# First norm's row factor moved behind the first projection, a new order around sine chains, filter banks, seam and cross heads

## The reference

```python
def first_block(x, ...):
    h = rmsnorm(x, norm_mix)                      # x * rsqrt(mean(x*x)) * gain, per position
    p = h @ w_in                                  # 2048 -> 4352: pool 512, hyena 3*768, gated MLP 2*768
    y_a = multiscale_pool_mixer(p[..., :512], ...)
    h_fwd, h_bwd = implicit_filters(...)          # two sine layers, then w3 times a decay table
    y_b = hyena_mixer(p[...], conv3, h_fwd, h_bwd, ...)   # width-3 convolution, long convolution by Fourier sums
    y_c = chunked_spatial_gating(p[...], ...)     # gelu, LayerNorm, 128x128 position mixing
    x = x + concat(y_a, y_b, y_c) @ w_out
    h = rmsnorm(x, norm_ffn)
    gate, val = split(dwconv3(h @ ffn_w_up))      # 2048 -> 11264
    x = x + (silu(gate) * val) @ ffn_w_down
    return rmsnorm(x, norm_final)

def hybrid_layer(x, mem, ...):                    # second block
    proj = rms_norm(x) @ w_in
    ya = chunked_band_attention(...)              # 8 heads
    yb = rwkv7_time_mix(...)                      # 16 heads, decay and rate from sigmoids of small products
    yc = memory_cross_attention(cq, mk, mv) * silu(cz)    # 4 heads of 256 against 256 memory rows
    return x + (sigmoid(ga)*(ya@w_up_a) + sigmoid(gb)*(yb@w_up_b) + sigmoid(gc)*(yc@w_up_c)) @ w_o
```

## Time and profile before

| | before |
|---|---|
| median of 3 runs (lowest to highest) | 2358.87 us (2358.87 to 2361.76) |
| the profiled execution, its own time | 2355.66 us |
| its span, first to last instruction | 2354.0 us |
| mean granted TensorE clock | 0.995 of full speed |
| PE busy | 2311.6 us, 98% |
| DVE busy | 1524.5 us, 65% |
| ACT busy | 1115.3 us, 47% |

### The profile page before, as it was taken

One profiled execution on the slowest core, in us unless ns is written; L12 is line 12 of the kernel. 1 busy time (PEld: TensorE's weight loads), 2 busy tenths in 40 slices (PEclk: granted clock), 3 DMA queues, 4 the chain that ended last, 5 costly groups with the idle time before them and its releaser, 6 DMA issues.

```text
span 2354.0 us, 54190 instructions
## 1 busy us (share of the span) xinstructions
PE 2311.6 (98%) x22128; PEld 2274.2 (97%) x22128; DVE 1524.5 (65%) x2096; ACT 1115.3 (47%) x1501; POOL 12.8 (1%) x27
## 2 busy tenths in 40 slices
PE   6999999999999999999999999999999899999999
PEld 6899999999999999999899999999998899999999
DVE  6657767666545666678676777777766555555554
ACT  5343445555434555444545555555545444444443
POOL 0000000000000000000000000000000000000000
PEclk9999999999999999999999999999999999999999
DMA  6453555555555555655554443443434355555554
GB/s 231 161 180 125 171 188 187 187 187 187 188 188 188 187 188 187 223 188 180 182 171 141 137 139 130 135 139 130 136 121 135 125 188 188 189 183 194 188 188 160
DMA packets 110245, 401.44 MB, mean 171 GB/s; under 512 B 12378, under 2 KB 12405, under 8 KB 109952
## 3 DMA queue, kind: packets, MB, share of 16 engines
q1 hardware_dynamic: 108000, 390.91, 50.4%
q0 software_dynamic: 2080, 8.06, 1.1%
HBM read 396.81 MB, written 2.10 MB: 169 GB/s over the span
## 4 chain that ended last, share of the span: by engine, by line
PE 97%; DVE 1%; ACT 1%; DMA 0%; issue 0%; SPq 0%; DVEq 0%; ACTq 0%
PE bank L465 97%; ACT w_hi L1085 0%; DVE w_lo L1617 0%; DMA x<-in_xT 0%; PE bank L893 0%; PE bank L994 0%; DVE croots L2405 0%; DVE scratch L1666 0%; DVE acc L1663 0%; PE bank L819 0%; DVE cstat L2414 0%; DVE cp L1669 0%; DVE h_lo L1663 0%; DVE root L1705 0%; DVE cqs L1666 0%
## 5 line engine op out<-in xcount | busy, mean ns | idle before, releaser
L1617 DVE TENSOR_TENSOR w_lo<-raw,w_hi 128x1024 fp32r<-128x1024 f32 x736 | 896.1, 1224 | 673.9 <-ACT w_hi L1085 666.6
L1085 ACT ACTIVATE w_hi<-raw 128x1024 fp32r<-128x1024 f32 x736 | 779.3, 1060 | 904.1 <-PE bank L465 900.0
L465 PE MATMUL bank<-h_hi,w_hi 128*128 128x256 f32 x4016 | 1137.0, 283 | 8.0 <-DVE h_lo L1663 8.0
L465 PE MATMUL bank<-h_lo,w_hi 128*128 128x256 f32 x4016 | 1124.3, 280 | 0.0
L465 PE MATMUL bank<-h_hi,w_lo 128*128 128x256 f32 x4016 | 1123.5, 280 | 0.0
L465 PEld LDWEIGHTS bank<-h_hi,w_hi 128*128 128x128 f32 x4016 | 758.9, 189 | 14.7 <-DVE h_lo L1663 8.7
L465 PEld LDWEIGHTS bank<-h_lo,w_hi 128*128 128x128 f32 x4016 | 759.0, 189 | 1.6
L465 PEld LDWEIGHTS bank<-h_hi,w_lo 128*128 128x128 f32 x4016 | 758.6, 189 | 0.0
L465 PE MATMUL bank<-m_hi,w_hi 128*128 128x256 f32 x704 | 196.5, 279 | 0.0
L465 PE MATMUL bank<-m_lo,w_hi 128*128 128x256 f32 x704 | 196.3, 279 | 0.0
L465 PE MATMUL bank<-m_hi,w_lo 128*128 128x256 f32 x704 | 196.3, 279 | 0.0
(11 more groups left out here) (426 smaller groups left out, 2737.8 us busy)
## 6 DMA issues: line engine op xcount, KB each, us to landing
raw<-in_units SPq DMA_DIRECT2D x736, 512.0 KB, 3.3
x<-in_xT SPq DMA_DIRECT2D x4, 512.0 KB, 5.9
memx<-in_memT POOLq DMA_DIRECT2D x4, 512.0 KB, 7.3
out_y<-obuf SPq DMA_DIRECT2D x8, 256.0 KB, 4.2
bias_t<-in_bias POOLq DMA_DIRECT2D x8, 192.0 KB, 2.7
dft<-in_dft POOLq DMA_DIRECT2D x1, 1024.0 KB, 7.8
decay<-in_decay POOLq DMA_DIRECT2D x1, 768.0 KB, 5.9
inv<-in_inv POOLq DMA_DIRECT2D x1, 512.0 KB, 3.7
```

What stands on the lines that cost most here:

```text
L465: return pe.matmul(out, lhsT, rhs, start=start, stop=stop, skip_group_check=True)
L1085: return act.activation(out, in_, ACT.Copy, scale=scale)
L1617: dve.tensor_tensor(w_lo[slot][:, :, :], raw[slot][:, :, :], w_hi[slot][:, :, :].bitcast(F32), ALU.subtract).then_inc(split_done, 1)
```

## The change

- **Head.** The row factor (one over the root, one number per position) commutes with the projection over channels. So `h_hi` is now x times gain rounded, made by ScalarE directly from x, and `h_lo` is x times gain minus `h_hi`, made by VectorE in one instruction per tile; neither waits for the sums. SP loads 16 columns of gains first, then x quarter 0, unit 0, quarter 1, unit 1 and so on, then the constants and the rest of the parameters. Squares and sums come with the second group's units; TensorE's `norm_sums` stands inside group 1. GpSimd's large tables wait for unit 7's landing, not unit 1's.
- **Banks read.** Every bank of the first projection is now read by VectorE with one multiplication by the row factor (`in_rows`, `pool_rows`, 128 x 512) into a buffer `scaled_in`, and the convolution and gelu read that. ScalarE's two copies of pool banks go. The LayerNorm has its own `ln_root`.
- **Sine chains.** The first sine chain comes before the root and before group 0's bank is read; the third group's units (8 to 11) are split one, one and two around them.
- **Filter products** use six banks: six in a row, then one unit, then the last two.
- **Seam.** The Sigmoid table is loaded right after `keys_root(3)`, and ScalarE's splits stand one before each pair of decays.
- **Cross heads.** On TensorE `scores(1)` to `scores(3)` and the transposes stand at other parts; ScalarE loads the Exp table right after a Silu; VectorE's `query_scaled` and `largest` stand between single splits.

```diff
+            def first_sums():
+                pe.wait_ge(tab_in, 32)
+                norm_sums(acc)
...
-            group(1, h_hi, h_lo, filled=False)
+            group(1, h_hi, h_lo, filled=False, then=(1, first_sums))
+            pe.wait_ge(ones_rounded, 1)
...
+            filter_products(0, 0, 1, 2, 3)
+            filter_products(1, 0, 1)
+            group(1, h_hi, h_lo, then=(0, banks_again))
+            from_dve(6)
...
             part(7)
+            scores(1)
             part(8)
-            scores(1)
             part(9)
+            weights_turned(1)
             part(10)
-            weights_turned(1)
+            scores(2)
             part(11)
-            scores(2)
             part(12)
-            part(13)
             weights_turned(2)
             scores(3)
+            part(13)
+            attended(0)
             part(14)
-            attended(0)
+            weights_turned(3)
             part(15)
-            weights_turned(3)
...
+            sp.dma_start(par[:, 0:KT], a["par"][:, 0:KT]).then_inc(gain_in, 16)
             for s in range(RING):
+                cs = slice(4 * s, 4 * s + 4)
+                sp.dma_start(x[:, cs, :], a["xT"][:, cs, :]).then_inc(x_in[s], 16)
                 sp.dma_start(raw[s][:, :, :], a["units"][s].rearrange("p (k n) -> p k n", k=UK))\
                     .then_inc(landed[s], 16)
+            sp.dma_start(con[:, :], a["con"]).then_inc(tab_in, 16)
+            sp.dma_start(par[:, KT:NPAR], a["par"][:, KT:NPAR]).then_inc(tab_in, 16)
...
+                for t in range(4 * c, 4 * c + 4):
+                    m = act.activation(h_hi[:, t, :], x[:, t, :], ACT.Identity, scale=col("norm_mix", t))
+                to_dve(m)
+                split()
...
             keys_root(3)
-            split4(2)
+            act.activation(spare[:, 0:1], con_("eps6"), ACT.Sigmoid)
+            split()
             decays(0)
             decays(1)
             split()
             decays(2)
             decays(3)
-            values_kept(0)
+            split()
             decays(4)
             decays(5)
+            values_kept(0)
             split()
...
+                for t in range(4 * c, 4 * c + 4):
+                    m = stt(h_lo[:, t, :], x[:, t, :], col("norm_mix", t), h_hi[:, t, :].bitcast(F32), ALU.mult,
+                            ALU.subtract)
+                to_pe(m)
+                split()
...
+                dst = scaled_last[:, :, :] if p == 16 else scaled_in[:, b, :, :]
+                read(tt(dst, p2(b), bcast(root[:, :], 2), ALU.mult), b)
...
-            split4()
+            sine("f_b1", "f_fr1")
+            split()
+            inverted(root)
             hyena(0)
-            sine("f_b1", "f_fr1")
-            split4()
+            split4(2)
+            sine("f_b2", "f_fr2")
             hyena(1)
-            sine("f_b2", "f_fr2")
             split4()
             hyena(2)
```

More of the change, by code:

```diff
@@ L1132, in high_halves, with in_rows @@
                     to_dve(copy(hi[:, cs, :], f[:, cs, :]))
-            squares(x, scratch, x_in)
+            act.wait_ge(gain_in, 16)
+            for c in range(4):
+                act.wait_ge(x_in[c], 16)
+                for t in range(4 * c, 4 * c + 4):
+                    m = act.activation(h_hi[:, t, :], x[:, t, :], ACT.Identity, scale=col("norm_mix", t))
+                to_dve(m)
+                split()
+            for quarters in ((0,), (1, 2), (3,), ()):
+                split()
+                for c in quarters:
+                    cs = slice(4 * c, 4 * c + 4)
+                    to_dve(act.activation(scratch[:, cs, :], x[:, cs, :], ACT.Square))
             act.wait_ge(tab_in, 32)
+            act.activation(spare[:, 0:1], con_("eps6"), ACT.Sqrt)
+            split()
+            root_of_mean(root[:, :], banks[2][:, 0:T])
             copy(ones_r[:, :], con_("ones"))
             copy(head_r[:, :], con_("head_ones")).then_inc(ones_rounded, 1)
-            act.activation(spare[:, 0:1], con_("eps6"), ACT.Sqrt)
-            root_of_mean(root[:, :], banks[2][:, 0:T])
-            high_halves(scratch, h_hi, with_units=True)
+            def in_rows(p):
+                n.next(("fill", p % 2))
+                act.wait_ge(bank_read[p % 2], n.now(("fill", p % 2)))
+                return scaled_last[:, :, :] if p == 16 else scaled_in[:, p % 2, :, :]
             def hyena(p):
@@ L1218, in _ @@
             psum()
-            to_dve(act.activation(root[:, :], banks[7][:, 0:T], ACT.Sqrt, bias=con_("eps5"), scale=1.0 / D_HY))
+            to_dve(act.activation(ln_root[:, :], banks[7][:, 0:T], ACT.Sqrt, bias=con_("eps5"), scale=1.0 / D_HY))
             split4()
@@ L1562, in _ @@
             gate_kept(0)
+            act.activation(spare[:, 0:1], con_("eps6"), ACT.Exp)
+            split()
+            softmax()
             split4(2)
+            weights_kept(0)
+            y_high(0)
+            split()
             softmax()
+            gate_kept(1)
+            act.activation(spare[:, 0:1], con_("eps6"), ACT.Exp)
             split()
-            weights_kept(0)
-            split()
-            gate_kept(1)
-            y_high(0)
-            split4(2)
-            softmax()
+            y_high(1)
             split()
@@ L1724, in running, with in_rows, pool_rows @@
                 settle()
+            dve.wait_ge(gain_in, 16)
             for c in range(4):
+                from_act()
+                for t in range(4 * c, 4 * c + 4):
+                    m = stt(h_lo[:, t, :], x[:, t, :], col("norm_mix", t), h_hi[:, t, :].bitcast(F32), ALU.mult,
+                            ALU.subtract)
+                to_pe(m)
+                split()
+            split4(2)
+            for c in range(3):
                 sum_quarter(c, scratch, acc)
+            split()
+            sum_quarter(3, scratch, acc)
+            split()
             dve.wait_ge(tab_in, 32)
-            inverted(root)
-            normalised(x, lambda t: col("norm_mix", t), scratch, h_hi, h_lo, root, with_units=True)
+            def in_rows(p):
+                b = p % 2
+                group_done()
+                n.next(("fill", b))
+                if p in (11, 12, 15):
+                    dve.wait_ge(gelu_done, {11: 1, 12: 2, 15: 3}[p])
+                dst = scaled_last[:, :, :] if p == 16 else scaled_in[:, b, :, :]
+                read(tt(dst, p2(b), bcast(root[:, :], 2), ALU.mult), b)
+            def pool_rows(p):
+                b = p % 2
+                group_done()
+                n.next(("fill", b))
+                read(tt(pool_x[:, 2 * (p - 13):2 * (p - 13) + 2, 8:8 + T], p2(b), bcast(root[:, :], 2), ALU.mult), b)
             def taps(dst, b, w0, w2):
-                o = p2(b)
+                o = scaled_in[:, b, :, :]
                 for s in range(2):
@@ L1749, in hyena @@
                 step(last[0]())
-                read(last[1](), b)
+                step(last[1]())
             def sine(b_, fr):
```

125 lines of the change are left out of this document (59 added, 66 removed).

## The result

The changed kernel takes **2319.46 us** (median of 4 runs, 2318.98 to 2319.83) against 2358.87 (four runs, 2357.88 to 2361.76): a ratio of 0.984, with an interval of 0.983 to 0.985. It is faster by 39.4 us in the medians.

The account below looks back on a forecast made before the run. TensorE, busy 98%, was taken as the bound, with its idle and low-clock time to be won: 11.5 + 6.2 - 0.4 + 7.2 + 14.3 = 38.8 us off 2355.66 gives 2316.9; from the median 2358.87, 2320. Range 2313 to 2332.

Parts of the forecast that it names:

- Head: Start of the kernel: first unit matmul at 10.4 instead of 22.97, less 1.0 for the sums; gain 11.5 us.
- Filter products: Filter stretch, 60.37 to 84.19: loss of 6.8 us from idle time and low clock, less 0.6; gain 6.2.
- the tie: Seventh filter product: TensorE there 6.9 us after group 2, its inputs ready after 6.7; 0.2 charged, at most 1.
- the even halves: Behind group 3: `even_kept` comes 4.4 us after the group's end, TensorE wants it after 4.0; 0.4 charged.
- the slower rival: Bank reading on VectorE comes too late, so all 17 groups pay; with 2.6 us each, 2364. Chance 2%.
- Cross heads: Cross-head stretch, 64.76 us long: loss of 15.1, less 0.5 and 0.3; gain 14.3, or 12 if head 2 is late.
- The nine steps: Cross heads, head 2's chain behind head 1's Exp, from loads to normalising: ready 1825.3, wanted 1825.4.
- The rule on table loads: Skill page: a table switch costs 2.66 us with drain, making head 2 2.8 late, gain 11.6; the forecast took 1.28.
- Clock low longer: Rival: up to 3 us more half speed at the start, or a clock fall at the filters; 2322 to 2327. Chance 12%.
- Head bound by loads: Rival: 512 KB pieces take 1.9 us instead of 1.28, unit 3 lands at 18.5; 2324. Chance 8%.
- Head 2 late: Rival, cross heads: two loads in one chain or a step longer than its row; 2322.5, or 2325 with clock fall. Chance 14%.
- Waits that re-form: Rival: waits return behind other semaphores in seam and cross heads, half of 7.2 + 14.3 lost; 2331. Chance 6%.

Follow-up runs that it names:

- the one with the old head: The kernel before with six filter banks, seam order and cross heads' order, so the changed kernel without new head and VectorE bank reading: 2326.96 us.
- the kernel without that wait: The changed kernel with two moves in the cross heads alone (Exp load behind the next split, y's second quarter behind head 2's softmax): 2317.95 us.
- one reading more: The changed kernel with VectorE doing each bank reading of the first projection twice, once for nothing: 2322.62 us.

## Why the prediction was right, point by point

- **Sum.** 38.8 was forecast against the profiled execution, 36.7 came: 2316.9 for 2318.98. The median came out at 2319.5 for 2320 since the profiled run of the kernel before lay 3.2 under its median, while the changed kernel's lay 0.5 under its own. That the median was met to 0.5 where the sum was 2.1 too high is luck.
- **Head, 11.5, measured 10.3.** The step that failed is "first matmul: 5.7 + 1.7 + 1.6 + 1.2 + 0.2 = 10.4": it came at 12.63. The sum has no term for the table load, 1.28 (shown by moving it); in the kernel before it had run at 0.88, out of the way. And x could be used at 6.56 in place of 5.7: I took the small load ahead of it at 0.4 and everything else at nothing. With that load on another queue x had landed by 5.8, so some 0.5 to 0.8 of the delay of 1.3 against 5.25 is that load's; the rest is open. The other three terms are right: scalings 1.71, VectorE's four 1.67, its split 1.22. "The first 13.45 us of PE I keep" was 12.54, which gave 0.9 back by luck: from the first matmul's start to the start of the 96th it took 12.61, and 13.69 in the changed kernel profiled again (12.73 to 26.42), by its longer slow start. The sums cost 1.0, as said. The place of the sums, "near 30.3", doesn't follow from its own terms: 10.4 + 5 + 5 x 2.8 = 29.4, so the margin was 1.4 and not 2. It held: the last addition ended at 28.97 and the sums started at 31.72.
- **Filter products, 6.2, measured 5.4.** Stretch 6.3 and the tie 0.2, as worked out; the even halves cost 0.9, not 0.4. ACT's timeline behind group 3, which ends at 67.59:

```profile
67.84 1.06 ACT L1098 ACTIVATE w_hi<-raw 128x1024 fp32r<-128x1024 f32 x1 [1.74 <-PE bank L471]
70.80 1.09 ACT L1178 ACTIVATE z<-scaled_in,par 128x256 f32<-128x256 f32 x2 [1.90 <-DVE scaled_in L1689]
71.79 0.84 ACT L1098 ACTIVATE k_re<-bank 128x384 f32<-128x384 f32 x2
```

  The chain is the one worked out (split, VectorE's split, reading, scaling, copy), but the first copy frees its bank for the product that starts at 72.31, 4.7 behind the group and not 4.4, and PE, by the spacing of its starts, would have been there after 3.9 and not 4.0: the handing over from engine to engine, four times, was in no term.
- **Bank reading, 0.4, measured 0.4** (PE waits 0.3 for `prod`, and behind the 24 units above the changed kernel takes 0.4 more to its end than the one with the old head: 2175.7 for 2175.3). But the reasons against the slower rival (work of 7.3 in 11.2) were an average. The experiments show no slack at all in the first three groups, and that the part would cost 2.2 more without the six banks.
- **Seam, 7.2, measured 7.3.** Loads and sigmoids where the prediction put them.
- **Cross heads, 14.3, measured 13.9.** The narrow head was head 2, as named, and its wait 1.4, or 1.7 in the length of the stretch, where 0.5 was charged. The nine steps were right: from the end of head 1's Exp (1788.80) to `cp` (1803.13) they took 14.3, which is what the forecast's terms add up to. Both ends were off. Counted from part 4, head 1's Exp ended 0.6 later than forecast, and PE was there at 1801.75, 0.9 earlier: a slack of 0.1 became a wait of 1.4. And the loss to be won was 15.6 (64.76 - 49.19, by the kernel without that wait) and not 15.1, which hid 0.5 of the error.
- **The rule on table loads.** Here the trace speaks against the Trainium skill, page "ScalarE: Activation LUTs", section "What ACT_TABLE_LOAD costs", which adds a drain of about 1380 ns to the load of 1283 ns. In the head the load ends at 7.84 and the scaling starts at 7.85. In the cross heads two loads stand in one chain without a drain:

```profile
1788.82 1.28 ACT L1564 ACT_TABLE_LOAD   x1
1790.11 0.60 ACT L1564 ACTIVATE czs<-bank 128x512 f32<-128x512 f32 x1
1790.73 1.28 ACT L1596 ACT_TABLE_LOAD   x1
1792.02 0.20 ACT L1596 ACTIVATE spare<-con 128x1 f32<-128x1 f32 x1
```

- **The rivals.** Clock low longer: the clock stayed at 1.00 at the filters and in the cross heads. Head bound by loads: no engine waited for unit 3. Head 2 late: it happened in small. Waits that re-form: refuted by PE's waits after the change and by the stretches of seam and cross heads.
- **The signs.** Three that the prediction named came out against it: the first matmul at 12.63 for 10.4; one wait for `cp` of 1.4, which was to be below 1; and unit 3 landing 10.5 us behind its issue at 5.58, so at 16.1, where "later than 15" was to be wrong. ACT came to unit 3 only at 17.10, so that limit had been set too tight.

## What to carry to other kernels

A wait of a few microseconds on a TensorE-bound kernel costs its length and then the clock: here 5.3 of idle time cost 7.9 and 9.3 cost 15.0, and even the 1.8 at the filters was followed by a clock of 0.79; a wait under 1.5 us cost about its length. A table load can end up behind the waits of the activation that needs it, as in the changed head, so look in the trace where it runs; if it stands on the path, give ScalarE a small activation ahead of the wait. And before adding work to an engine at 65%, follow it through the groups where it has no idle time: the average slack says nothing of them, and one part of a change can be what hides another.

## What the runs showed of the hardware that was not expected

- The half-speed stretch behind one and the same wait is not of one length: 2.9 and 5.7 us in the cross heads, 3.3 and 6.9 at the seam. Nor is the one at the start, in one and the same kernel: 3.3 and 5.4. Why it differs wasn't tried.
- A table load isn't bound to one side of its activation's wait: at 0.88, ahead of it, in the kernel before, and at 6.56, behind it, in the changed one.
- A unit of 24 matmuls takes 2.80 or 2.82 us on average, with a granted clock of 1.00 both times and no idle time. It holds for long stretches: 0.65 us over 24 units above, and in one run (one reading more) with 2329.3 where the others of its kernel have 2321.4 to 2327.8, these two windows of 3003 matmuls, first that run, then the changed kernel:

```profile
390.33:743.67 353.34, 353.34 (x3003) 353.34 (x3002) 215.70 (x275) 164.81 (x206) 0.00 (x0) 1.00 0.56 186
```
```profile
386.15:736.15 350.00, 350.00 (x3003) 350.00 (x3001) 215.59 (x275) 165.25 (x206) 0.00 (x0) 1.00 0.57 188
```

  Half of what that run has above its kernel's median lies in this window alone. What sets the two rates wasn't tried.
